# Late sums behind the states, halves exchanged by ScalarE, and gated rows transposed one job later in a retention stage

## The reference

```python
q = _rotary(q, pos) * (dk ** -0.5)       # 4 heads, dk = dv = 128
k = _rotary(k, pos)
scores = einsum('bnchd,bnshd->bnhcs', qc, kc) * intra_decay
o = einsum('bnhcs,bnshe->bnche', scores, vc)
U = einsum('bnshd,bnshe->nbhde', kc * k_decay, vc)
R_i = chunk_decay * R_(i-1) + U_i        # a scan over blocks of positions
o = o + einsum('bnchd,nbhde->bnche', qc * q_decay, R_prev)
ro = _head_norm(o) * silu(rg)            # the gated rows
```

## Time and profile before

| | |
|---|---|
| median of 3 runs | 2864.9 us (2857.21 to 2865.62) |
| the profiled execution's own time | 2864.02 us |
| its span | 2862.2 us |
| PE busy | 2673.2 us (93%) |
| DVE busy | 1450.6 us (51%) |
| ACT busy | 947.6 us (33%) |
| POOL busy | 692.3 us (24%) |
| mean granted TensorE clock | 0.967 of full |

### The profile page before, as it was taken

How to read it: one execution, slowest core, us unless ns; L and a number is a source line. 1 busy time by engine, 2 the same in 40 slices (tenths; PEclk the granted TensorE clock), 3 DMA queues, 4 the chain that set the end, 5 groups by cost and what they waited for, 6 DMA issues and landing times.

```text
span 2862.2 us, 34000 instructions
## 1 busy us (share of the span) xinstructions
PE 2673.2 (93%) x13340; PEld 1384.3 (48%) x13340; DVE 1450.6 (51%) x2298; ACT 947.6 (33%) x1120; POOL 692.3 (24%) x355
## 2 busy tenths in 40 slices
PE   6988999888999999999988899888999999999998
PEld 3666767544344444444454444344544444444443
DVE  6254444566644455475575748754335722222225
ACT  3322333225233233233353344233425322332331
POOL 1210214111221222131631312116112812221222
PEclk9989999999999999999989899999999999999999
DMA  7311121301111111130112212011011201111111
GB/s 300 122 47 59 45 108 45 103 30 59 59 58 31 59 59 46 48 128 30 45 60 74 72 65 95 7 67 30 30 45 35 83 30 59 59 42 47 59 45 59
DMA packets 55589, 182.44 MB, mean 64 GB/s; under 512 B 3952, under 2 KB 4368, under 8 KB 48016
## 3 DMA queue, kind: packets, MB, share of 16 engines
q1 hardware_dynamic: 47136, 138.89, 14.4%
q10 hardware_dynamic: 8304, 41.46, 4.0%
HBM read 170.90 MB, written 9.45 MB: 63 GB/s over the span
## 4 chain that ended last, share of the span: by engine, by line
PE 74%; DVE 10%; ACT 4%; DVEq 3%; POOLq 3%; issue 2%; DMA 1%; POOL 1%; ACTq 1%; SPq 0%
PE PS L681 22%; PE PS L682 22%; PE PS L683 22%; DVE XT L2076 1%; POOLq L610 1%; POOLq L608 1%; PE PS L723 1%; DMA Hf<-in_w_ada 1%; PE PS L1423 1%; ACT WB L1490 1%; POOL WB L554 1%; DVEq L2075 1%; PE PS L1396 1%; ACT WS L1492 1%; PE PS L972 1%
## 5 line engine op out<-in xcount | busy, mean ns | idle before, releaser
L554 POOL TENSOR_TENSOR WB<-WS,WB 128x512 f16<-128x512 f32 (+1 forms) x264 | 494.1, 1903 | 1892.3 <-ACT WS L1492 1892.0
L681 PE MATMUL PS<-XT,WB 128*128 128x512 f16 x1568 | 599.3, 382 | 17.8 <-DVE Hf L2074 12.1
L682 PE MATMUL PS<-XT,WB 128*128 128x512 f16 x1568 | 598.7, 382 | 0.0
L683 PE MATMUL PS<-XT,WB 128*128 128x512 f16 x1568 | 598.5, 382 | 0.0
L681 PE MATMUL PS<-WB,Hf 128*128 128x512 f16 x1440 | 551.2, 383 | 20.7 <-DVEq L2079 6.4
L682 PE MATMUL PS<-WB,Hf 128*128 128x512 f16 x1440 | 550.8, 383 | 0.0
L683 PE MATMUL PS<-WB,Hf 128*128 128x512 f16 x1440 | 550.4, 382 | 0.0
L2074 DVE CAST Hf<-S 128x512 f16<-128x512 f32 x172 | 146.0, 849 | 482.1 <-ACT S L1734 387.0
L1490 ACT ACTIVATE WB<-WS 128x2048 f16<-128x2048 f32 (+3 forms) x118 | 212.5, 1801 | 505.5 <-PE PS L683 468.9
L2438 DVE SCALAR_TENSOR_TENSOR R<-PS,R 128x512 f32<-128x512 f32 x208 | 143.0, 691 | 261.1 <-PE PS L683 252.8
L681 PEld LDWEIGHTS PS<-XT,WB 128*128 128x128 f16 x1568 | 154.4, 98 | 205.1 <-DVE Hf L2074 7.8
(11 more groups left out here) (377 smaller groups left out, 2780.4 us busy)
## 6 DMA issues: line engine op xcount, KB each, us to landing
WS<-in_w_ff SPq DMA_DIRECT2D x32, 1024.0 KB, 5.1
WS<-in_mlp_w SPq DMA_DIRECT2D x32, 1024.0 KB, 5.2
WS<-in_w_mix SPq DMA_DIRECT2D x20, 1024.0 KB, 4.9
Hf<-in_w_ada ACTq DMA_DIRECT2D x12, 1024.0 KB, 5.8
Hf<-in_w_ada SPq DMA_DIRECT2D x8, 1024.0 KB, 10.7
WS<-in_w_out SPq DMA_DIRECT2D x8, 1024.0 KB, 5.1
R<-in_x SPq DMA_DIRECT2D x4, 1024.0 KB, 9.4
R<-in_x ACTq DMA_DIRECT2D x2, 2048.0 KB, 8.0
```

What stands on the lines that cost most here:

```text
L554: op = pool.tensor_tensor(WB[:, slot, 1, at:at + n], WS[:, hf, i * n:(i + 1) * n], WB[:, slot, 0, at:at + n], ALU.subtract)
L681: pe.matmul(o, ah, bh, start=(first and k == 0), stop=False, skip_group_check=True)
L682: pe.matmul(o, ah, bl, start=False, stop=False, skip_group_check=True)
L683: mm = pe.matmul(o, al, bh, start=False, stop=(last and k == n - 1), skip_group_check=True)
```

## The change

Four edits, all in the retention stage.

1. `late_sum(h+2)` is no longer cut in halves around the states: all of it comes behind them.
2. ACT writes q and k a second time with the halves exchanged, straight from PSUM (two more instructions of 64 partitions x 512 for each of jobs 0 to 3), into `sw` and a new unit `swk`; `rotate` loses its four copies. `swk` is R's unit 6, which the next stage's gates use later, so ACT waits for `rot` of head 3 ahead of `gates(1)`.
3. `rotate` does its four multiplications first and then the two additions.
4. The transposes of head h's gated rows move from behind job 7 to behind job 0 of the next iteration (`gated_rows(h - 1)`); for head 3 they stay.

```diff
         RU.update({n: unit(R, i) for n, i in dict(qd=0, kn=1, a=2, rs=3, on=4, g1=5).items()})
+        RU["sw"], RU["swk"] = unit(S, 4), unit(R, 6)
...
+            def gated_rows(h):
+
+                pe.wait_ge(mix_v, mv_ret(h, "gated"))
+                for g in range(2):
+                    b = side_bank()
+                    for u in range(4):
+                        n = (4 * g + u) * P
+                        mm = pe.transpose(PS[:, b, u * P:(u + 1) * P], RU["on"][:, n:n + P], IDENT)
+                    side_end(mm)
...
                     if j == 0:
+                        if h >= 1:
+                            gated_rows(h - 1)
                         late_total(h + 1)
                         pe.wait_ge(mix_v, mv_ret(h, "rot"))
...
                             for jj in range(4):
                                 project_job(wide(C["gla0"]), jj)
-                        pe.wait_ge(mix_v, mv_ret(h, "gated"))
-                        for g in range(2):
-                            b = side_bank()
-                            for u in range(4):
-                                n = (4 * g + u) * P
-                                mm = pe.transpose(PS[:, b, u * P:(u + 1) * P], RU["on"][:, n:n + P], IDENT)
-                            side_end(mm)
+                            gated_rows(h)
...
-                        dst = RU["qr"] if j < 2 else RU["kr"]
-                        act.activation(dst[:, (j % 2) * HALF:(j % 2 + 1) * HALF], PS[:, b, :],
-                                       ACT.Copy, scale=UNSCALE).then_inc(evac[b], 1)
+                        dst, turned = (RU["qr"], RU["sw"]) if j < 2 else (RU["kr"], RU["swk"])
+                        c = slice((j % 2) * HALF, (j % 2 + 1) * HALF)
+                        act.activation(dst[:, c], PS[:, b, :], ACT.Copy, scale=UNSCALE)
+                        act.activation(turned[0:64, c], PS[64:128, b, :], ACT.Copy, scale=UNSCALE)
+                        act.activation(turned[64:128, c], PS[0:64, b, :], ACT.Copy,
+                                       scale=UNSCALE).then_inc(evac[b], 1)
...
                 if not nxt:
+                    act.wait_ge(mix_v, mv_ret(3, "rot"))
                     gates(1)
...
-                for raw, dst in (("qr", "qh"), ("kr", "kh")):
+                for raw, turned, dst in (("qr", "sw", "qh"), ("kr", "swk", "kh")):
+                    dve.tensor_tensor(RU[turned], RU[turned], RU["sin"], ALU.mult)
+                    dve.tensor_tensor(RU[dst], RU[raw], RU["cos"], ALU.mult)
+                for turned, dst in (("sw", "qh"), ("swk", "kh")):
                     dve.drain()
-                    dve.tensor_copy(RU["sw"][0:64, :], RU[raw][64:128, :])
-                    dve.tensor_copy(RU["sw"][64:128, :], RU[raw][0:64, :])
-                    dve.drain()
-                    dve.tensor_tensor(RU["sw"], RU["sw"], RU["sin"], ALU.mult)
-                    dve.tensor_tensor(RU[dst], RU[raw], RU["cos"], ALU.mult)
-                    dve.drain()
-                    dve.tensor_tensor(RU[dst], RU[dst], RU["sw"], ALU.add)
+                    dve.tensor_tensor(RU[dst], RU[dst], RU[turned], ALU.add)
...
                 late_evac(h + 1)
-                if h < 3:
-                    late_sum(h + 2, (0,))
                 for g in range(2):
                     K[0] = ret_side(h, "u", g)
...
                 dve.drain().then_inc(mix_v, 1)
                 if h < 3:
-                    late_sum(h + 2, (1,))
+                    late_sum(h + 2)
```

More of the change, by code:

```diff
@@ L2173, in late_evac, with late_sum @@
                     mod_diagonal(4 + i)
-            def late_sum(i, halves=(0, 1)):
-                for j in range(4 * halves[0], 4 * halves[-1] + 4):
+            def late_sum(i):
+                for j in range(8):
                     if j % 4 == 0:
@@ L2185, in late_sum @@
                         dve.scalar_tensor_tensor(LATE_SUM, w, f, LATE_SUM, ALU.mult, ALU.add)
-                if halves[-1]:
-                    dve.drain().then_inc(late_summed, 1)
+                dve.drain().then_inc(late_summed, 1)
             def columns_half(hf, dst):
```

## The result

The changed kernel takes 2833.66 us (median of 4 runs, 2832.42 to 2834.35) against 2864.07 (4 runs, 2857.21 to 2865.62) for the kernel before: 30.4 us less, ratio 0.9898 with a 95% interval of 0.9881 to 0.9915. The forecast was 2835.5 us, a gain of 29.1.

A forecast was written before the change was run, and what follows sets the result against it. PE, busy 93% of the span, was taken as the bound, so only its idle or slowly clocked time counts. Gains of 23.4 and 5.7 us sum to 29.1, giving 2835.5 us, range 2825 to 2846.

The forecast's parts named there:

- The late sum: Outputs of heads 0 to 2 stop waiting for the states: 23.4 us, 15.5 of waiting and 7.9 of clock.
- What is queued behind it: DVE's norm, gating and rotation start 2.7 to 3.9 us late, covered by the 4.50 us root wait: cost 0.
- ScalarE's halves and the rotation: ACT's copies of 0.6 us hidden; DVE's rotation about 7.4 us; scores' wait gone, gaining 5.7 us in iteration 1.
- The gated rows' move: Transposes moved behind job 0 are done before ACT's rounding ends, so they don't hold kt up: 0.
- Kt in iterations 0 and 2: Kt's second half stays 12.8 us after job 7, held by ACT's rounding: gain 0, bounds -1.1 to +2 each.
- the low clock behind it stays too: PE's low clock behind kt's wait was to remain in iterations 0 and 2, gain 0.
- A: Longer light work behind job 0 makes PE's clock fall earlier or longer: 5 us lost, 2840.5 us; chance 0.13.
- B: Less rotation load on DVE brings kt earlier in iterations 0 and 2, about 5 us each: 2825.5 us; chance 0.09.
- C: Clock loss in the outputs isn't given back, only waits go: gain 19 us, 2845.5 us; chance 0.09.
- D: Late sum's DMA lands some 14 us late, delaying rotation so scores wait: over 2865 us; chance 0.03.
- E: Outputs wait for something other than the states, so that wait stays: 2859 us from iteration 1 alone; chance 0.03.

The follow-up runs named there:

- Run 2: The changed kernel with the late sum cut in halves around the states again: 2856.19 us, ratio 0.9981.
- run 1: The kernel before with one edit, the late sums whole behind the states: 2835.96 us, ratio 0.9916.
- Run 8: The changed kernel with ACT writing the first exchanged half three times, a drain behind each: 2834.96 us, ratio 0.9906.
- run 7: The changed kernel with the late DMAs of iterations 0 to 2 issued some 8.7 us later, behind job 4's copy: 2851.98 us, ratio 0.9964.
- run 4: The changed kernel without ACT's two additional copies, halves exchanged by DVE's copies and the old rotation order: 2836.98 us, ratio 0.9913.
- run 11: The kernel of run 5 with the halves exchanged by DVE's copies and the old rotation: 2829.78 us, ratio 0.9882.
- run 3: The changed kernel with the gated rows' transposes behind job 7 again: 2832.95 us.
- run 5: The kernel of run 3 with ACT scaling the gated rows ahead of rounding the next chunk: 2823.57 us, ratio 0.9870.
- run 6: The changed kernel, gated rows still transposed behind job 0, with ACT scaling them ahead of rounding: 2823.52 us, ratio 0.9869.
- run 9: The changed kernel timed and profiled once more, unchanged: 2832.06 us, ratio 0.9894.
- run 10: The changed kernel again, unchanged, for a third profile: 2832.2 us in a single run.

## Why the prediction was right

**The late sum (forecast 23.4 us).** From the updates' start to the outputs' end the changed kernel takes 15.6 us in heads 0 to 2; head 3 as a template had given 15.7. By the profiles 23.5 us are gained, waits and clock both, as forecast. Run 2 gives 22.5 back; run 1 has 26.7, of which 1.7 us are iteration 0's clock by its profile. This is most of the change.

**What is queued behind it (forecast 0).** Right: the statistics start 3.0 us behind the outputs' end (2.7 to 3.9 forecast), and the root's wait shrinks to 1.56 us. Run 8 used it up at no loss to speak of, run 7 went past it and paid.

**ScalarE's halves and the rotation (forecast hidden on ACT; gain in iteration 1 only).** Right: 0.59 us each, rotation 7.2 us for 7.4. Iteration 1 gained 5.4 us from the outputs' end to the next updates (41.1 to 35.7), for a forecast of 5.7. Runs 4 and 11 show the wait of 3.7 us that returns without it.

**The gated rows' move (forecast 0).** Right by run 3. The reason given was ACT's rounding, which ends after either place. That fits the rows, but it isn't the only cover: in runs 5 and 6, with the scaling first, both places are as good too.

**Kt in iterations 0 and 2 (forecast 0, bounds -1.1 to +2 each).** Here the step was in part wrong. Kt's second half comes 12.0 us after job 7, not 12.8: the first cast takes 0.66 us, not 1.42, by how it falls on POOL's subtractions. And "the low clock behind it stays too" was wrong as a rule. It stays, goes or doubles between executions of one kernel (runs 9 and 10). In the first profile iteration 0 gained 2.5 us (my bound was 2) and iteration 2 lost 0.5. Each is about 0.8 us from the cast, and the rest is, roughly, the clock: 1.7 us of work less lost in iteration 0, 1.7 more in iteration 2. That these two cancelled is luck. It leaves 2.0 us for the two iterations, where I had 0, and 7.4 us in all behind the outputs, against 5.7.

**The rivals.** A (more light work, more clock loss) saw the right quantity, but run 3 gives it no support as a consequence of the change. B (kt earlier since DVE is freed) fell: kt waits as long as before with 2.8 us of copies gone from each rotation. Its sum of 2825.5 us is close to what runs 5 and 6 reach, but by ACT's order and by casts clear of POOL. C fell by clocks of 1.00 in the outputs. D was no danger at the DMA's actual landing (4.7 us after issue), and its price was too low: run 7 lost 18.3 us for 8.7 us of lateness, where my own terms give 3 x (8.7 - 4.2) = 13.5. At three us for each further one, slower than before would begin near 13 us of lateness rather than 14; that was not tried. E fell with runs 1 and 2.

## What to carry to other kernels

Put work that waits for a DMA behind the short work that another engine waits for, and look for what covers it in that place: here a wait of 4.50 us for another engine's root. When load is taken off an engine, look at each of its idle rows for who ends them: DVE's 1.00 us of waiting for ACT said that a faster rotation would buy nothing there, and it also named the edit that did, swapping two blocks in ACT's order, worth 8.5 to 10 us (runs 5 and 6, at 2823.6 and 2823.5 us the best versions run). Price a delay together with what it will be beside: the same rotation takes 7.2 us before POOL starts and 10.7 to 11.1 us beside it (run 7).

## What was not expected of the hardware

The half clock behind a short stall isn't repeatable. With the same instructions and waits (2.7 us idle in two pieces among light matmuls) three profiles of one kernel show 0, 1.7 or 3.4 us of work lost to it; with the wait removed (runs 5 and 6) there was no fall in these places. It makes a period of one kernel differ by up to 3 us between executions (57.4 against 54.5). The runs of run 1, whose kernel keeps its waits in three iterations, spread over 9.6 us with mean clocks of 0.970 to 0.973; this fits, but only one of them was traced, so it isn't shown.

DMAs issued on ACT's queue behind three copies left beside the first one (137.24 beside 137.23 us), so the change's two more copies didn't delay them. In run 8, with two more copies again and a drain behind each, they left 2.6 us behind the first copy (140.15 against 137.53), and the late sum starts 14.4 us behind the updates' start instead of 11.7. More copies without drains were not run there.
